# Gathered experts: neighbouring weight rows on each partition, and a gather with every eighth feature on its left

## The reference, cut to what matters

```python
def grouped_moe(x, router_w, router_bias, w_gate, w_up, w_down):
    xt = x.reshape(-1, d)
    ...                                    # router: two experts of 16 for each token, and their weights
    y = jnp.zeros(xt.shape, dtype=jnp.float32)
    for e in range(N_EXPERTS):
        he = jax.nn.silu(xt @ w_gate[e]) * (xt @ w_up[e])
        y = y + combine[:, e:e + 1] * (he @ w_down[e]).astype(jnp.float32)
    return y
```

## Time and profile before

| | us |
|---|---|
| median of 3 runs | 2599.98 (2597.93 to 2602.13) |
| profiled execution | 2603.51 |
| its span in the trace | 2601.7 |
| PE busy | 2431.6 (93%) |
| DVE busy | 1674.4 (64%) |
| ACT busy | 1178.4 (45%) |
| mean granted clock of PE, of full speed | 0.972 |

### The profile page before, as it was taken

The page is one execution under the profiler, slowest core; times in us unless marked ns, Lnnn a source line. Parts: engine busy times, 40 slices in busy tenths (PEclk is TensorE's granted clock), DMA queues, the critical chain, the costliest instruction groups (busy, mean ns, idle before and its releaser), DMA issues.

```text
span 2601.7 us, 38914 instructions
## 1 busy us (share of the span) xinstructions
PE 2431.6 (93%) x14366; PEld 1990.5 (77%) x14366; DVE 1674.4 (64%) x2114; ACT 1178.4 (45%) x1447; POOL 104.0 (4%) x82
## 2 busy tenths in 40 slices
PE   9999999999999989999999889999998897999997
PEld 8998787998998878799876778975544686976543
DVE  5665766666666675666544665668776546668776
ACT  5554423444554532344422334456664332446663
POOL 0000141000000032000000000000000000000000
PEclk9999999999999999999998999999998997999998
DMA  6667303555567620365553334678895432578884
GB/s 196 179 199 215 109 1 98 168 181 174 174 180 221 185 66 1 116 191 179 182 176 105 114 113 124 192 254 307 307 314 187 141 107 81 171 233 314 308 311 168
DMA packets 386970, 458.11 MB, mean 176 GB/s; under 512 B 18542, under 2 KB 273170, under 8 KB 386706
## 3 DMA queue, kind: packets, MB, share of 16 engines
q1 hardware_dynamic: 381824, 446.35, 54.0%
q10 hardware_dynamic: 5010, 9.98, 1.3%
HBM read 451.56 MB, written 1.05 MB: 174 GB/s over the span
## 4 chain that ended last, share of the span: by engine, by line
PE 48%; issue 36%; DVE 11%; ACT 3%; POOL 2%; SPq 0%; DMA 0%; ACTq 0%; POOLq 0%; DVEq 0%; PEldq 0%
PE PS L1952 3%; PE PS L1954 3%; PE PS L1953 3%; PE PS L2059 3%; PE PS L2061 2%; PE PS L2060 2%; DVE wlo L1793 2%; PE PS L2154 2%; PE PS L1969 2%; PE PS L1970 2%; PE PS L1971 2%; PE PS L2156 1%; PE PS L2155 1%; ACT whi L785 1%; PE PS L2078 1%
## 5 line engine op out<-in xcount | busy, mean ns | idle before, releaser
L1180 DVE TENSOR_TENSOR wlo<-raw,whi 128x1024 fp32r<-128x1024 f32 x336 | 409.7, 1223 | 299.2 <-ACT whi L738 296.2
L738 ACT ACTIVATE whi<-raw 128x1024 fp32r<-128x1024 f32 x336 | 353.6, 1055 | 360.2 <-PE PS L1954 291.5
L1952 PE MATMUL PS<-xTh,whi 128*128 128x256 f32 x1792 | 508.7, 284 | 6.5 <-DVE xTl L1147 4.7
L1954 PE MATMUL PS<-xTh,wlo 128*128 128x256 f32 x1792 | 507.8, 283 | 0.0
L1953 PE MATMUL PS<-xTl,whi 128*128 128x256 f32 x1792 | 507.7, 283 | 0.0
L1952 PEld LDWEIGHTS PS<-xTh,whi 128*128 128x128 f32 x1792 | 344.2, 192 | 12.5 <-DVE xTl L1147 5.7
L1953 PEld LDWEIGHTS PS<-xTl,whi 128*128 128x128 f32 x1792 | 344.2, 192 | 3.9
L1954 PEld LDWEIGHTS PS<-xTh,wlo 128*128 128x128 f32 x1792 | 344.3, 192 | 0.0
L1793 DVE TENSOR_TENSOR wlo<-raw,whi 128x1024 fp32r<-128x1024 f32 x188 | 222.2, 1217 | 34.6 <-ACT whi L785 34.4
L785 ACT ACTIVATE whi<-raw 128x1024 fp32r<-128x1024 f32 x188 | 190.9, 1051 | 44.3 <-PE PS L2061 15.8
L2154 PE MATMUL PS<-whi,xTh 128*128 128x416 f32 (+2 forms) x480 | 183.7, 383 | 17.7 <-DVE xTl L1147 7.5
(11 more groups left out here) (473 smaller groups left out, 4504.3 us busy)
## 6 DMA issues: line engine op xcount, KB each, us to landing
raw<-in_l_e_gate_dram SPq DMA_DIRECT2D x128, 512.0 KB, 5.1
raw<-in_l_e_up_dram SPq DMA_DIRECT2D x128, 512.0 KB, 6.0
raw<-in_l_e_down_dram SPq DMA_DIRECT2D x128, 512.0 KB, 4.9
raw<-in_ffn_w_gate_dram SPq DMA_DIRECT2D x88, 512.0 KB, 5.3
raw<-in_ffn_w_up_dram SPq DMA_DIRECT2D x88, 512.0 KB, 6.2
raw<-in_ffn_w_down_dram SPq DMA_DIRECT2D x88, 512.0 KB, 3.4
raw<-in_w_in_dram SPq DMA_DIRECT2D x64, 416.0 KB, 4.1
raw<-in_l_xkv_dram SPq DMA_DIRECT2D x32, 512.0 KB, 3.8
```

The lines of the kernel that those rows point to most:

```text
L738: nc.scalar.activation(whi[:, m if slot is None else slot], raw[:, m, j], ACT.Copy).then_inc(hi_done[m], 1)
L1180: nc.vector.tensor_tensor(wlo[:, w], raw[:, m, j], whi[:, w].bitcast(F32), ALU.subtract).then_inc(lo_done[m], 1)
L1952: mm(out_, whi[:, m, ks], xTh[:, k, :], start=(k == 0), stop=False)
L1954: last = mm(out_, wlo[:, m, ks], xTh[:, k, :], start=False, stop=(k == KB - 1))
```

## The change

The gate and up weights of the 13 gathered experts are laid out so that partition `p` holds the eight neighbouring rows 8p to 8p + 7; chunk `c` brings rows 8p + 2c and 8p + 2c + 1, which lie side by side in memory. To match, block `k` of the gathered activations has to hold features 8p + k: the gather's left operand, 128 values long as before, now takes every eighth feature of `xrh` or `xrl`, a step of 32 bytes from one value to the next.

```diff
                         for m in ("e_up", "e_gate"):
                             for c in range(4):
-                                expert_load(w[m][at_e[i % 2]].rearrange("o (k p) f -> p (o k) f", p=P)[:, 2 * c:2 * c + 2, :], 2)
+                                expert_load(w[m][at_e[i % 2]].rearrange("o (p k) f -> p (o k) f", p=P)[:, 2 * c:2 * c + 2, :], 2)
...
-                    rows = xrl if u % 2 else xrh
+                    rows = (xrl if u % 2 else xrh)[:].rearrange("p t (m k) -> p t k m", k=KB)
                     for t in range(NT):
-                        last = mm(PS[:, UNIT_BANKS[u % 6], 0:c1 - c0], rows[:, t, u // 4 * P:(u // 4 + 1) * P], pick[:, t, c0:c1], start=(t == 0), stop=(t == 1))
+                        last = mm(PS[:, UNIT_BANKS[u % 6], 0:c1 - c0], rows[:, t, u // 4], pick[:, t, c0:c1], start=(t == 0), stop=(t == 1))
```

## The result

| | us |
|---|---|
| before, median of 20 runs | 2597.86 (2590.02 to 2602.15) |
| after, median of 20 runs | 2607.02 (2598.83 to 2615.85) |
| ratio after / before | 1.0035, 95% interval 1.0023 to 1.0046 |
| after, span of the profiled execution | 2598.0 |

The change makes the kernel slower by 0.35%, about 9 us. The two profiled spans say the opposite, 2598.0 after against 2601.7 before, and are no evidence: single executions of one kernel lie 12 to 17 us apart here. The profiles are read only for the stages that the change touches.

A forecast was written before the change was run, and what follows sets the result against it. PE, busy for 93% of the span, was taken as the bound, its gathered-stage waits being for DVE. Loads 0 plus gather 0 left the profiled 2603.5, less 3.5 to the runs' median: 2600.0 us, range 2593 to 2608.

The forecast's parts named there:

- rival (a): Gather's stepped weight load takes twice as long (214 ns), 0.226 us per matmul, +5.7 us, 2606; chance 0.11.
- PE waits for DVE's order, not for loads; a cheaper transfer is worth 0.: Gathered experts: PE's short waits, 10.9 us in 13, are all for DVE, so cheaper gate and up loads save 0 us.
- Packets near 20500, DMA share 0.887 to about 0.863, a landing 0.16 us shorter.: Gathered experts' DMAs, 1725 to 1965 us: 4 KB pieces cut packets from 32250, with busy share and landing time slightly lower.
- the 2.7% of the sum: Gathered experts' DMAs: predicted saving in time per byte from fewer pieces per KB, bounded from two mixes of packets.
- rival (c): Gathered experts' new reading order slows DMAs, deciding beyond an 11% lower rate; at 15%, +23 us, 2623; chance 0.05.
- (d): DMAs limit the gathered experts' stage; if all ACT's waits for DMAs went away, 17 us faster, 2583; chance 0.07.
- (e): Gathered experts' load pieces stay 2 KB, as two descriptors side by side; same time, 2600; chance 0.10.
- The gather's load may grow 1.6 times before it shows.: Gather: the weight load may grow from 107 to about 170 ns, hidden under the matmul before it, 0 us.
- The stepped load takes no more than 1.6 times as long, by DVE's line 1707.: Gather: stepped load judged by a DVE row whose 64 byte jumps cost 5 ns or nothing; 0 us.
- A load asks for values slowly enough (0.84 ns each) to hide a new line with each.: Gather: a load asks for values nearly as slowly as DVE (1.04 ns), half as fast as a matmul's right operand (0.43).
- (b): Gather's stepped load takes four times as long or more, 0.440 us per matmul, +33 us, 2633, up to +88; chance 0.07.

The follow-up runs named there:

- The run at 108.8% and 311 GB/s: Gathered experts' gate and up loads in 512 byte pieces, same bytes in four times as many pieces, against the kernel before; ratio 1.0001.

## Why the prediction was right and wrong

The time, 2607.0, lies in the stated range (2593 to 2608), near its end. The forecast itself, the median unchanged, was wrong; rival (a) is what happened, and it had a chance of 0.11. The range holds the time because it was drawn wide enough for (a), and with some luck: the median of before over 20 runs is 2597.86, 2.1 us under the 2600.0 that I went by, and the same 0.35% on top of 2599.98 would have been 2609.

- *PE waits for DVE's order, not for loads; a cheaper transfer is worth 0.* The forecast held: loads in 4 KB pieces alone gave 0.9994. That loads aren't waited for is shown by the 512 B pieces, 1.0001 with longer landings; the 4 KB pieces didn't land earlier, so they don't test it.
- *Packets near 20500, DMA share 0.887 to about 0.863, a landing 0.16 us shorter.* The packets were right. The share in the layer 0 window was 88.4% at 310 GB/s; per byte the fall was 1.1% and 2.8% in the two layers against the 2.7% of the sum, not clear of the scatter of 1.3%. The landing did not get shorter. The sum also took the busy share for a measure of capacity (rates of 298 and 346 GB/s at full share). The run at 108.8% and 311 GB/s shows that it isn't one, and rival (c)'s turning point of 11%, drawn from it, has no ground.
- *Rivals (c) and (d), the loads cost or save time, and (e), the pieces stay 2 KB:* out, by the loads alone at 0.9994, the unchanged stages, and the 20402 packets.
- *The gather's load may grow 1.6 times before it shows.* Not contradicted: with halved matmuls a load side by side fits in 0.112 us, and with a step of 8 bytes the slightly longer record (195 ns) left the pace at 0.183. No run had a load between 0.112 and 0.236 us, so the 1.6 itself was not tried.
- *The stepped load takes no more than 1.6 times as long, by DVE's line 1707.* This is the step that failed. The load takes about 0.24 us against 107 to 112 ns, 2.2 times, so it sets the gather's pace: 8.0 us where I put 0. The row that stood for it read PSUM, its neighbours in the comparison read SBUF, and its 64 values hop between two places. A reduction with one step of 64 bytes throughout cost DVE 38% more from SBUF, and the stepped splits cost DVE and ACT about twice the time per value.
- *A load asks for values slowly enough (0.84 ns each) to hide a new line with each.* Wrong: side by side, DVE's split takes 1.1 ns a value and ACT's 0.94, both slower than the load, and both took about twice as long with the step.
- *Rival (a): twice as long, 0.226 us per matmul, +5.7 us.* It is what happened: a load of about twice the length sets the pace. The term was short: it measures 0.244 us per matmul, 8.0 us. By the rule, the traces agree: the Trainium skill (Advanced Engine Details and Errata, section SBUF Cachelines) asks for two hits on a line of 16 bytes, and the cliff between steps of 8 and 16 bytes, 0.183 against 0.236 us, lies just there. I had priced that rule and then given it 0.18 with (b) against a row that didn't bear on it. That a line of 16 bytes is the cause, and not merely where the cliff lies, is the Trainium skill's account; no run here looks inside the memory.
- *Rival (b), four times and more:* out. Beyond one value per 16 bytes the price hardly grows, 0.236 to 0.244.

## What to carry to other kernels

In fp32, a step in an operand that is read from SBUF can have a price for whoever reads it. A weight load of 128 columns took a step of 8 bytes for nothing, and steps of 16 or 32 bytes cost it its 0.11 us over again and more. So where the transfer only needs longer pieces, neighbouring rows grouped in pairs give them without that price. Before making a transfer cheaper, see who waits for it; here the DMA engines were busy for 89% of the time in the gathered stage, and a landing a microsecond later changed nothing for PE. And a row taken as the nearest has to share the memory and the pattern of the thing that it stands for.

## What the runs showed of the hardware

- A weight load of 128 fp32 columns with a step of 32 bytes sets a pace of 0.24 us whatever PE's clock: 0.239 at a granted clock of 1.00 and 0.240 at 0.50 within one gather, and 0.244 at 1.00 in the changed kernel. With steps of 4 or 8 bytes it stays hidden under 0.18 us, with 16 bytes the pace is 0.236.
- Stepped reads of fp32 from SBUF (32 bytes) take DVE's split 2.0 ns a value against 1.1 and ACT's 2.1 against 0.94. A reduction on DVE with a step of 64 bytes pays 0.63 ns a value from SBUF and nothing from PSUM (425 against 424 ns for 256 values).
- The busy share of the DMA engines can pass 100% (108.8% at 311 GB/s) where it was 88.7% at 307, without a longer stage. Packets of 4 KB in place of 2 KB lowered it by 0.6 to 2.8% per byte, with a scatter of 1.3% between kernels of the same pieces.
